# Up-projections of a hybrid decoder trunk as three fp32r products of rounded and low parts

## The chip, the cores and the metric

The kernel runs on one core of one Trainium2 chip. The metric is the device time of one launch in microseconds (us). PE is TensorE, PEld its weight loads, ACT is ScalarE, DVE is VectorE, POOL is GpSimd and SP is SyncE, which issues nearly all DMAs. A line such as L886 is a line of the kernel before.

## What is computed

A step of a two-layer recurrent decoder over 512 prompt tokens and 8 sample tokens (520 columns, held as two halves of 260). Each layer normalizes its input, projects it to four token mixers (A: RWKV-7, B: retention, C: RG-LRU, D: gated delta) and to 4 x 1024 merge-gate columns, runs the mixers, and merges them:

```python
h = rms_norm(x, lp['norm_g']) * (1.0 + scale[:, None]) + shift[:, None]
proj = jnp.einsum('btd,de->bte', h, lp['w_in'])
# oA, oB, oC, oD: mixer outputs, (tokens, 256) each, gated by silu of their own columns
branches = jnp.stack([oA, oB, oC, oD], axis=2)
up = jnp.einsum('btnw,nwd->btnd', branches, lp['w_up'])        # w_up: (4, 256, 1024)
gl = proj[..., OFF_G:].reshape(B, T, N_BRANCH, D_MODEL)
merged = jnp.sum(jax.nn.sigmoid(gl) * up, axis=2)
out = merged @ lp['w_out']
x_new = x + gate[:, None] * out
```

`up` is what the change touches. In each layer it is 4 branches x 8 column tiles = 32 tiles, each a 256-deep product for 128 output columns and 520 tokens.

## The kernel before

Everything lies channel-major: 128 channels on the partitions, 520 tokens along the free axis. Five engines run instruction lists written out by hand; one engine waits for another by a semaphore at a numbered step, and each engine works strictly in the order of its list. `L.tiles` gives the order of the weight tiles, and SP issues loads in the same order.

The large products (`proj` and `gate` tiles, the `out` tiles, and `ada`, the conditioning projection) are already computed from parts. `split` on ACT rounds a weight tile of 128x1024 to fp32r (L1436), POOL subtracts that from the tile in two halves of 128x512 (L708), and PE adds hi x hi, hi x lo and lo x hi (L836, L844) in 48 fp32r matmuls of 260 columns. The up tile idx (`up`, L877 to L888) is different: 4 matmuls in plain fp32 straight from the loaded weights `upw` (three buffers, `UP_RING`) and the mixer output in `RA`, `RB`, `RC` or `RD`. The trace shows two records for each such matmul, so 8 for an up tile. DVE then multiplies the result in PSUM by 1 + tanh of the gate and adds it to the merged sum (`merged`, L1888 to L1906: L1900 for idx below 8, else L1903 and L1904). Products on PSUM bank pairs alternate, so an up tile needs the pair that was used two tiles before. The tanh tiles of the gates are stashed in DRAM and brought back (`stash`, `bring_back`), again by SP.

The 32 up tiles of a layer are computed in three places. Tiles 0 to 7 (branch A) lie between gate tiles 8 to 15, while DVE and ACT prepare branch D: `first_out` and `gated(0)` finish branch A (L2063 to L2070, L1917 to L1921) in the middle of D's convolution (`conv`, L2079), after which come ACT's tanh (L1646), D's silu (L2097), a log series (`log1p`, L1825 to L1837) and a scan (L2108), for which PE waits at L1145. Tiles 8 to 17 (D and the first two of C) lie around the retention loop (`for c in range(NCB)`, L1326 to L1342 on PE), with two up tiles after each chunk and then the next gate tile. Tiles 18 to 31 (the rest of C, and B) are the tail of the layer: they alternate with `ada` tiles (14 of them in layer 0, 8 in layer 1), whose weights are 512 KB each; DVE merges, and for idx above 24 it also takes the low part of a merged tile (`m_lo`, L1886) after ACT has rounded it (`m_hi`, L1790). The `out` products follow. In the tail ACT's order is: for i in 0 to 13, `mod_rows(i)` (which splits the ada tile four ahead, once its load has landed) and from i = 7 on `m_hi(i - 7)`.

Of the kernel before, what the change touches and what calls it, by code (L numbers as in the profile page):

```python
# [18 lines left out]
P = 128  # L19
KT = D_MODEL // P  # L20
# [57 lines left out]
def build_program(nc, a, o, order):  # L78
# [8 lines left out]
    with ctx:  # L87
        def sb(name, shape, dt=F32):
            return ctx.enter_context(nc.sbuf_tensor(name, shape, dt))
# [22 lines left out]
        RC = sb("RC", [P, 4, TT])  # L112
# [4 lines left out]
        upw = sb("upw", [P, RING, 2, P])  # L117
# [8 lines left out]
        cT = sb("cT", [P, KT, 9])  # L126
# [15 lines left out]
        svA = sb("svA", [P, 6, NB, 2])  # L142
        svB = sb("svB", [P, 8, NB, 2])
        rowA = prow
        vecA = vecB = sb("vec", [P, 8, HD])
        vv = sb("vv", [P, 3, 16])
        so = sb("so", [P, 3, 16])
# [69 lines left out]
        class Layer:  # L217

            def __init__(self, n):
# [12 lines left out]
                    "pe_n", "act_n", "dve_n", "pe_m", "act_m", "dve_m")}  # L232
# [228 lines left out]
        for layer, L in enumerate(LAYERS):  # L461
# [354 lines left out]
            def _(pe):  # L816
# [50 lines left out]
                outs = (RA[:, 2:4, :], RB[:, 4:6, :], RC[:, 0:2, :], RD[:, 4:6, :])  # L867

# [68 lines left out]
                nc.tensor.transpose(psB[0:96, 0, 0:P], svA[:].rearrange("p n b i -> p (n b i)"), ident).then_inc(*ps_.step("rows"))  # L937
# [485 lines left out]
            def _(act):  # L1423
# [138 lines left out]
                def after_fill():  # L1562
                    evacs(fill_a.ends_in(next(slots)))
# [251 lines left out]
            def _(dve):  # L1815
# [247 lines left out]
                def first_out():  # L2063
# [6 lines left out]
                    gated(0, outs3[0], RA[:, 7:9, :])  # L2070

# [468 lines left out]
```

## Time and profile before

| | us |
|---|---|
| three runs | 1541.17, 1542.26, 1546.21 |
| median | 1542.26 |
| the profiled execution | 1549.12 |
| its span, first to last instruction | 1547.3 |

The profiled execution is 6.9 us over the median. PE is busy for 1429.0 us of the span (92%), DVE for 648.0, ACT for 519.4, POOL for 473.8; the granted clock of TensorE is 0.962 on average. An engine's busy share is a mean over the whole span. Whether a shorter product helps depends on who is awaited where it stands, so the time is read by the stretches of a layer. Layer 0's tiles 0 to 7 lie from 369 to 438 us, tiles 8 to 17 from 591 to 661 us and tiles 18 to 31 from 676 to 724 us; layer 1 repeats it some 750 us later.

### The profile page before, as it was taken

What the parts mean: (1) busy time and instruction counts of PE and PEld (TensorE: products, weight loads), DVE (VectorE), ACT (ScalarE), POOL (GpSimd) and SP (SyncE); (2) the same over time, 40 slices, a digit from 0 to 9 for tenths busy, and PEclk for the clock granted to TensorE, in tenths of its full rate; (3) what the DMA queues carried; (4) which work ended last, traced back from release to release, by engine and by line L of the source; (5) the groups of instructions that cost most, each with busy time, mean ns of one, the idle gap of its engine ahead of it and who ended that gap; (6) DMA issues with size and microseconds to landing.
All of it is one profiled execution on the core that took longest, in us unless ns stands there. A gap on an engine that the chain in (4) does not pass through costs nothing.

```text
span 1547.3 us, 33515 instructions
## 1 busy us (share of the span) xinstructions
PE 1429.0 (92%) x14880; PEld 1292.1 (84%) x14880; DVE 648.0 (42%) x1115; ACT 519.4 (34%) x780; POOL 473.8 (31%) x350
## 2 busy tenths in 40 slices
PE   6799999999899999897979999999999999989896
PEld 4699999888789888775879998998888988877695
DVE  5625313317732436545123541141494242563432
ACT  5524322234422234144333252221542123514322
POOL 0244322223221122157633442122422122212720
PEclk9899999999899999998999999999998999999998
DMA  9532321225231354477543323122352126246811
GB/s 319 192 92 67 83 64 49 57 56 120 74 95 41 66 112 122 94 244 230 162 127 95 82 68 83 43 56 56 83 126 82 43 57 118 75 117 169 274 43 55
DMA packets 275908, 162.18 MB, mean 105 GB/s; under 512 B 86102, under 2 KB 244922, under 8 KB 275252
## 3 DMA queue, kind: packets, MB, share of 16 engines
q1 hardware_dynamic: 274100, 159.06, 37.7%
q8 instruction: 117, 1.92, 0.5%
q10 hardware_dynamic: 1664, 0.98, 0.3%
q14 instruction: 27, 0.22, 0.0%
HBM read 135.25 MB, written 24.89 MB: 103 GB/s over the span
## 4 chain that ended last, share of the span: by engine, by line
PE 75%; DVE 14%; ACT 4%; issue 3%; DMA 2%; SPq 1%; POOL 0%; ACTq 0%; DVEq 0%
PE psA L836 31%; PE psA L844 15%; PE psA L886 5%; PE psB L772 3%; PE psB L781 3%; PE psB L782 2%; PE psB L717 1%; DVE RA L1930 1%; DVE ws L2079 1%; PE psB L959 1%; DMA RB<-in_ada_w 1%; PE psB L969 1%; DVE ws L1833 1%; PE psB L1145 1%; PE psB L1402 1%
## 5 line engine op out<-in xcount | busy, mean ns | idle before, releaser
L708 POOL TENSOR_TENSOR w_lo<-ring,w_hi 128x512 fp32r<-128x512 f32 (+1 forms) x274 | 382.2, 1417 | 956.8 <-ACT w_hi L1436 896.3
L836 PE MATMUL psA<-h_hi,w_hi 128*128 128x260 f32 x1984 | 430.9, 299 | 21.0 <-DVE h_lo L1848 12.8
L836 PE MATMUL psA<-h_lo,w_hi 128*128 128x260 f32 x1984 | 406.5, 287 | 0.0
L836 PEld LDWEIGHTS psA<-h_hi,w_hi 128*128 128x128 f32 x1984 | 312.6, 193 | 39.3 <-issue 19.8
L836 PEld LDWEIGHTS psA<-h_lo,w_hi 128*128 128x128 f32 x1984 | 312.9, 192 | 0.2
L844 PE MATMUL psA<-h_hi,w_lo 128*128 128x260 f32 x1984 | 275.2, 288 | 0.0
L844 PEld LDWEIGHTS psA<-h_hi,w_lo 128*128 128x128 f32 x1984 | 251.5, 189 | 4.6 <-issue 0.3
L1436 ACT CAST w_hi<-ring 128x1024 fp32r<-128x1024 f32 x133 | 137.2, 1033 | 33.3 <-PE psA L844 18.4
L787 ACT COPY ws<-psB 128x128 f32<-128x128 f32 x80 | 21.5, 268 | 246.5 <-PE psB L772 246.5
L795 DVE COPY_PREDICATED tg<-tmask,psB 128x128 f32<-128x128 uint8 x40 | 14.3, 356 | 137.5 <-PE psB L782 97.5
L1465 ACT ACTIVATE tg<-psA 128x520 f32<-128x520 f32 x48 | 28.9, 601 | 101.4 <-PE psA L844 101.2
L795 DVE COPY_PREDICATED ws<-tmask,psB 128x128 f32<-128x128 uint8 x40 | 14.3, 357 | 86.4 <-PE psB L782 51.2
L2323 DVE SCALAR_TENSOR_TENSOR xT<-psA,modT,xT 128x260 f32<-128x260 f32 x16 | 7.8, 489 | 97.2 <-PE psA L844 97.2
L708 POOL TENSOR_TENSOR w_lo<-ring,ra_lo 128x512 fp32r<-128x512 f32 x28 | 36.5, 1329 | 29.1 <-ACT ra_lo L1436 29.1
L886 PE MATMUL psA<-RB,upw 128*128 128x260 f32 x128 | 35.9, 434 | 8.4 <-DVE RA L1904 6.8
L886 PEld LDWEIGHTS psA<-RB,upw 128*128 128x128 f32 x128 | 27.1, 217 | 16.0 <-DVE RA L1904 7.3
L782 PE MATMUL psB<-tg,ws 64*64 64x32 f32 x640 | 38.0, 221 | 0.0
L782 PE MATMUL psB<-ws 64*64 64x32 f32 x640 | 37.4, 220 | 0.0
L886 PE MATMUL psA<-RA,upw 128*128 128x260 f32 x128 | 32.2, 399 | 4.4 <-DVE RA L1921 4.4
L708 POOL TENSOR_TENSOR rb_lo<-RB,ra_lo 128x512 fp32r<-128x512 f32 x20 | 25.5, 1303 | 31.9 <-ACT ra_lo L1436 31.9
L1762 ACT COPY RB<-psB 64x256 f32<-64x256 f32 x16 | 5.9, 367 | 85.3 <-PE psB L1342 85.2
L782 PEld LDWEIGHTS psB<-tg,ws 64*64 64x64 f32 x640 | 32.6, 137 | 1.1
(476 smaller groups left out, 2349.8 us busy)
## 6 DMA issues: line engine op xcount, KB each, us to landing
ring<-in_w_in SPq DMA_DIRECT2D x122, 512.0 KB, 4.1
scr_tanh<-tg SPq DMA_DIRECT2D x48, 260.0 KB, 4.5
ring<-in_ada_w SPq DMA_DIRECT2D x18, 512.0 KB, 4.3
upw<-in_w_up SPq DMA_DIRECT2D x64, 128.0 KB, 3.9
RA<-scr_tanh SPq DMA_DIRECT2D x30, 260.0 KB, 4.0
RB<-in_ada_w SPq DMA_DIRECT2D x14, 512.0 KB, 5.1
ws<-scr_tanh SPq DMA_DIRECT2D x24, 260.0 KB, 4.2
ring<-in_w_out SPq DMA_DIRECT2D x9, 512.0 KB, 4.6
```

Source lines behind the costliest of these rows:

```text
L708: nc.gpsimd.tensor_tensor(tile_part(RL[s][:, k], (kind, n)), tile_part(RS[s][:, k], (kind, n)), tile_part(HS[L.hslot[q]][:, k], (kind, n)) ...
L717: last = nc.tensor.matmul(psB[:, k, 0:HALF], bones, s4[:, k, :], start=True, stop=True)
L772: last = nc.tensor.matmul(meet(psB[sd(g), 2, q * CH:(q + 1) * CH], lv, 0), At[sd(g), q, :], meet(T4[sd(g), q, :], lv, 0), start=True, stop ...
L781: nc.tensor.matmul(meet(psB[sd(g), 2, q * CH:(q + 1) * CH], lv, 0), V4[sd(g), q, :], meet(Y4[sd(g), q, :], lv, 0), start=True, stop=True)
L782: last = nc.tensor.matmul(meet(psB[sd(g), 2, 256 + q * CH:256 + (q + 1) * CH], lv, 1), Y4[sd(g), q, :], meet(V4[sd(g), q, :], lv, 1), star ...
L787: nc.scalar.copy(meet(q64(Y), lv, 0), meet(q64(psB[:, 2, 0:256]), lv, 0)).then_inc(*ta.step("y"))
L795: nc.vector.copy_predicated(meet(q64(T), lv, 0), bc(meet(tmask[:, lv, :], lv, 0), 1, 4), meet(q64(psB[:, 2, 0:256]), lv, 0))
L836: nc.tensor.matmul(out(h), HS[L.hslot[q]][:, p, 0:m], cols(part(p), h), start=(p == 0 and part is hi), stop=False)
L844: last = nc.tensor.matmul(out(h), RL[s][:, k, 0:m], cols(hi(k), h), start=False, stop=(k == KT - 1))
L886: last = nc.tensor.matmul(out(hf), upw[:, idx % UP_RING, i, :], outs[MERGE[idx][0]][:, i, hf * HALF:(hf + 1) * HALF], start=(i == 0), stop ...
L1436: nc.scalar.copy(tile_part(HS[L.hslot[q]], SPLIT[q]), tile_part(RS[s], SPLIT[q])).then_inc(*aw.step("hi"))
L1465: A(half(th_tile(idx)), psA[:, b:b + 2, 0:HALF], ACT.Tanh, scale=0.5).then_inc(*am.step("th"))
```

## The change

`up` becomes three fp32r products, as the large tiles have them: 12 matmuls instead of 4. Their operands are new tiles: `up_hi` (weights rounded by ACT), `up_lo` (weights less `up_hi`, written over `upw`), and for each branch `out_hi` (ACT) and `out_lo`, each 128x1040, written behind the branch's gate.

- ACT rounds up weights 0 to 2 at the end of stage A (ahead of `mrow`), 3 to 20 behind the gate tiles of `ups_after`, and 21 to 31 in the tail, each behind `mod_rows(i)` and ahead of `m_hi`. From idx 3 on it waits for the load and for the up tile three before. It rounds the branch outputs behind gates 9, 23 and 28 and at i = 1 in the tail, ahead of the next `split`.
- POOL takes the low part of up weights 0 to 20 and of branch outputs 1 to 3, each ahead of one of its own gate or ada tiles. For branch 3 that is ada tile 5.
- DVE takes the low part of branch output 0, directly behind `gated(0)`, after waiting for ACT. In the tail it takes the low parts of up weights 21 to 31, each directly behind the merge three tiles before.
- To make room, some small tiles share memory: `svA` with `svB`, and `vv`, `so` and `cT` with each other.

```diff
-        upw = sb("upw", [P, RING, 2, P])
+        upw, uplo = sb_parts("upw", "up_lo", [P, RING, 2, P])
+        uphi = sb("up_hi", [P, RING, 2, P], F32R)
...
+            out_f = (RA[:, 2:4, :], RD[:, 4:6, :], RC[:, 0:2, :], RB[:, 4:6, :])
+            out_hi = (wsr[:, 8:10, :], mhi[:, 6:8, :], RClo[:, 2:4, :], RBr[:, 6:8, :])
+            out_lo = (RAlo[:, 2:4, :], mhi[:, 4:6, :], RClo[:, 0:2, :], RBr[:, 4:6, :])
+            ON_DVE = 21
...
+            ups_after = {10: (3,), 11: (4,), 12: (5,), 13: (6,), 14: (7,), 22: (8,), 23: (9,), 24: (10,), 25: (11,), 26: (12,),
+                         27: (13, 14), 28: (15, 16), 29: (17, 18), 30: (19, 20)}
+            outs_after = {9: (0,), 23: (1,), 28: (2,)}
+            two_on = lambda g: SPLIT[SPLACE["gate", g] + 2]
+            UPS_AT = {two_on(g): idxs for g, idxs in ups_after.items()}
+            UPS_AT[two_on(8)] = (0, 1, 2)
+            OUTS_AT = {two_on(g): bs for g, bs in outs_after.items() if g != 9}
+            OUTS_AT["ada", 5] = (3,)
...
             def _(pool):
                 for q, (kind, n) in enumerate(SPLIT):
                     s, _ = ring_slot(kind, n, L)
+                    for idx in UPS_AT.get((kind, n), ()):
+                        pool.wait_ge(*TR["act_u"].at("uhi", idx))
+                        nc.gpsimd.tensor_tensor(uplo[:, up_slot(idx)], upw[:, up_slot(idx)], uphi[:, up_slot(idx)], sub).then_inc(*pu.step("ulo"))
+                    for b in OUTS_AT.get((kind, n), ()):
+                        pool.wait_ge(*an.at("ohi", b))
+                        nc.gpsimd.tensor_tensor(out_lo[b], out_f[b], out_hi[b], sub).then_inc(*pu.step("olo"))
...
                 def up(idx):
-                    if idx in (0, 8, 16, 24):
-                        pe.wait_ge(*dn.at("gated", idx // 8))
+                    b, first = idx // 8, idx % 8 == 0
+                    if first:
+                        pe.wait_ge(*an.at("ohi", b))
                     psum_free("up", idx)
-                    pe.wait_ge(L.up[idx % UP_RING], 16 * (idx // UP_RING + 1))
-                    out = psum("up", idx)
+                    pe.wait_ge(*TR["act_u"].at("uhi", idx))
+                    out, s = psum("up", idx), up_slot(idx)
+                    for x in (out_hi[b], out_lo[b]):
+                        if x is out_lo[b] and first:
+                            pe.wait_ge(*(pu.at("olo", b - 1) if b else dn.at("olo")))
+                        for i in range(2):
+                            for hf in range(2):
+                                nc.tensor.matmul(out(hf), uphi[:, s, i, :], x[:, i, hf * HALF:(hf + 1) * HALF], start=(i == 0 and x is out_hi[b]), stop=False)
+                    pe.wait_ge(*low_at(idx))
                     for i in range(2):
                         for hf in range(2):
-                            last = nc.tensor.matmul(out(hf), upw[:, idx % UP_RING, i, :], outs[MERGE[idx][0]][:, i, hf * HALF:(hf + 1) * HALF],
-                                                    start=(i == 0), stop=(i == 1))
+                            last = nc.tensor.matmul(out(hf), uplo[:, s, i, :], out_hi[b][:, i, hf * HALF:(hf + 1) * HALF], start=False, stop=(i == 1))
                     last.then_inc(*pm.step("gate"))
...
+                def up_split(idx):
+                    act.wait_ge(L.up[up_slot(idx)], 16 * (idx // UP_RING + 1))
+                    if idx >= UP_RING:
+                        act.wait_ge(*pm.at("gate", idx - UP_RING))
+                    nc.scalar.copy(uphi[:, up_slot(idx)], upw[:, up_slot(idx)]).then_inc(*TR["act_u"].step("uhi"))
+                def out_split(b):
+                    act.wait_ge(*dn.at("gated", b))
+                    nc.scalar.copy(out_hi[b], out_f[b]).then_inc(*an.step("ohi"))
...
                         A(half(th_tile(idx)), psA[:, b:b + 2, 0:HALF], ACT.Tanh, scale=0.5).then_inc(*am.step("th"))
+                        for b in outs_after.get(idx, ()):
+                            out_split(b)
+                        for k in ups_after.get(idx, ()):
+                            up_split(k)
...
+                for idx in range(3):
+                    up_split(idx)
                 act.wait_ge(*pa.at("mt"))
...
                     if i < n_ada:
                         mod_rows(i)
+                    if i == 1:
+                        out_split(3)
+                    if 21 + i < 32:
+                        up_split(21 + i)
                     if i >= 7:
                         m_hi(i - 7)
...
                             T_(half(mg[j]), up, half(mg[j]), add).then_inc(*dm.step("mg"))
+                        if idx + 3 >= ON_DVE and idx + 3 < 32:
+                            s = up_slot(idx + 3)
+                            dve.wait_ge(*TR["act_u"].at("uhi", idx + 3))
+                            T_(uplo[:, s], upw[:, s], uphi[:, s], sub).then_inc(*du.step("ulo"))
...
                     gated(0, outs3[0], RA[:, 7:9, :])
+                    dve.wait_ge(*an.at("ohi", 0))
+                    T_(out_lo[0], out_f[0], out_hi[0], sub).then_inc(*dn.step("olo"))
```

## Rows read from the trace of the kernel before

**Rows 1.** The page: busy time of engines (part 1), chain of waits (part 4).

```profile
PE 1429.0 (92%) x14880; PEld 1292.1 (84%) x14880; DVE 648.0 (42%) x1115; ACT 519.4 (34%) x780; POOL 473.8 (31%) x350
PE 75%; DVE 14%; ACT 4%; issue 3%; DMA 2%; SPq 1%; POOL 0%; ACTq 0%; DVEq 0%
```

**Rows 2.** Windows: stretch, length, busy us, granted clock, DMA share, GB/s.

```profile
369.00:411.00 42.00, 36.11 (x248) 33.42 (x248) 38.67 (x48) 20.12 (x17) 13.55 (x9) 0.98 0.60 135
...
676.30:702.00 25.70, 23.31 (x106) 15.77 (x105) 11.04 (x16) 10.76 (x13) 22.35 (x18) 1.00 0.95 316
702.00:734.00 32.00, 22.04 (x88) 15.56 (x88) 20.26 (x23) 14.30 (x19) 25.52 (x18) 0.78 0.66 212
```

**Rows 3.** Timeline of PE, an up tile between gate tiles: start, us, idle before.

```profile
374.74 2.08 PE L844 MATMUL psA<-h_hi,w_lo 128*128 128x260 f32 x16
376.66 1.92 PE L886 MATMUL psA<-RA,upw 128*128 128x260 f32 x8
```

**Rows 4.** Timelines of ACT and PE, end of stage A.

```profile
343.63 1.04 ACT L1436 CAST w_hi<-ring 128x1024 fp32r<-128x1024 f32 x1
344.57 0.36 ACT L1629 COPY mrow<-psB 64x256 f32<-64x256 f32 x1
...
345.81 1.99 PE L717 MATMUL psB<-RA,cst 128*128 128x260 f32 x8 [1.62 <-ACT crow L1634]
```

**Rows 5.** Timelines of DVE and POOL around `gated(0)`.

```profile
358.98 1.24 DVE L2065 TENSOR_TENSOR RA<-RA,ws 128x1040 f32<-128x1040 f32 x1 [5.47 <-ACT ws L1488]
...
366.79 2.19 DVE L1921 SCALAR_TENSOR_TENSOR RA<-RA,ws 128x1040 f32<-128x1040 f32 x1
369.02 5.97 DVE L2079 SCALAR_TENSOR_TENSOR ws<-RD,parT,ws 128x510 f32<-128x510 f32 x6
...
360.39 7.49 POOL L708 TENSOR_TENSOR w_lo<-ring,w_hi 128x512 fp32r<-128x512 f32 x4 [13.14 <-ACT w_hi L1436]
```

**Rows 6.** Timelines of DVE, POOL and PE on to L1145.

```profile
397.18 0.69 DVE L1833 TENSOR_TENSOR ws<-ws 4x520 f32<-4x520 f32 x1
398.36 1.67 DVE L1833 TENSOR_TENSOR ws<-ws 4x520 f32<-4x520 f32 x1
...
398.16 3.02 POOL L708 TENSOR_TENSOR w_lo<-ring,w_hi 128x512 fp32r<-128x512 f32 x2 [6.37 <-ACT w_hi L1436]
...
411.23 3.75 PE L1145 MATMUL psB<-bg,cst 4*128 4x512 f32 x4 [4.49 <-DVE bg L2108]
```

**Rows 7.** Timelines of PE and ACT, second place and the gate before it.

```profile
573.16 0.60 PE L836 MATMUL psA<-h_hi,w_hi 128*128 128x260 f32 x2 [0.39 <-ACT ws L1732]
...
626.10 0.69 PE L1337 MATMUL psB<-ws,M 64*64 64x128 f32 x4 [4.11 <-DVE ws L2269]
...
644.76 3.67 PE L886 MATMUL psA<-RD,upw 128*128 128x260 f32 x16
...
645.73 0.60 ACT L1465 ACTIVATE tg<-psA 128x520 f32<-128x520 f32 x1
```

**Rows 8.** Up weight loads, issue to landing: up to 676 us, then 682 to 712.

```profile
DMA to landing us min/median/max: 2.2/3.3/5.0
...
DMA to landing us min/median/max: 3.8/6.4/7.7
```

**Rows 9.** Timelines of ACT, POOL, PE and DVE in the tails.

```profile
691.67 1.04 ACT L1436 CAST w_hi<-RB 128x1024 fp32r<-128x1024 f32 x1 [5.41 <-DMA RB<-in_ada_w]
...
690.19 2.53 POOL L708 TENSOR_TENSOR rb_lo<-RB,ra_lo 128x512 fp32r<-128x512 f32 x2
...
694.46 0.62 PE L1372 MATMUL psB<-rb_lo,c_parts 128*18 128x512 f32 x2
702.02 1.99 PE L886 MATMUL psA<-RB,upw 128*128 128x260 f32 x8 [0.39 <-DMA upw<-in_w_up]
...
711.74 1.34 DVE L1886 TENSOR_TENSOR ra_lo<-RA,merged_hi 128x520 fp32r<-128x520 f32 x1 [0.97 <-ACT merged_hi L1790]
1471.86 0.69 DVE L1886 TENSOR_TENSOR merged_lo<-mg,merged_hi 128x520 fp32r<-128x520 f32 x1
```

More of the change, by code:

```diff
@@ L111, in build_program @@
         RB, RBr = sb_parts("RB", "rb_lo", [P, 8, TT])
-        RC = sb("RC", [P, 4, TT])
+        RC, RClo = sb_parts("RC", "rc_lo", [P, 4, TT])
         RD, mhi = sb_parts("RD", "merged_hi", [P, 8, TT])
@@ L125, in build_program @@
         G = sb("G", [P, KT, 9])
-        cT = sb("cT", [P, KT, 9])
         chl = sb("c_parts", [P, KT, 18], F32R)
@@ L141, in build_program @@
         crowA = mg5[0:11, 2:4, :].rearrange("p a b -> p (a b)")[:, 0:7 * P]
-        svA = sb("svA", [P, 6, NB, 2])
         svB = sb("svB", [P, 8, NB, 2])
+        svA = svB[:, 0:6]
         rowA = prow
         vecA = vecB = sb("vec", [P, 8, HD])
-        vv = sb("vv", [P, 3, 16])
-        so = sb("so", [P, 3, 16])
+        decode_small = sb("decode_small", [P, 96])
+        vv, so = (decode_small[:, 48 * k:48 * k + 48].rearrange("p (n v) -> p n v", n=3) for k in range(2))
+        cT = decode_small[:, 0:72].rearrange("p (k s) -> p k s", k=KT)
         sa = sb("sa", [P, 2, 16])
@@ L231, in __init__ @@
                     "pe_c", "act_c", "dve_c", "pe_s", "act_s", "dve_s", "pe_p", "act_p", "act_w", "pool_w",
-                    "pe_n", "act_n", "dve_n", "pe_m", "act_m", "dve_m")}
+                    "act_u", "pool_u", "dve_u", "pe_n", "act_n", "dve_n", "pe_m", "act_m", "dve_m")}
                 self.n_ada = 24 if n == 0 else 8
@@ L476, in ada_bank, with low_at @@
                 return 2 if b in (1, 3) else 1
+            pu, du = TR["pool_u"], TR["dve_u"]
+            out_f = (RA[:, 2:4, :], RD[:, 4:6, :], RC[:, 0:2, :], RB[:, 4:6, :])
+            out_hi = (wsr[:, 8:10, :], mhi[:, 6:8, :], RClo[:, 2:4, :], RBr[:, 6:8, :])
+            out_lo = (RAlo[:, 2:4, :], mhi[:, 4:6, :], RClo[:, 0:2, :], RBr[:, 4:6, :])
+            up_slot = lambda idx: idx % UP_RING
+            ON_DVE = 21
+            def low_at(idx):
+                return pu.at("ulo", idx) if idx < ON_DVE else du.at("ulo", idx - ON_DVE)
             def merged_at(idx):
@@ L865, in proj @@
                         last.then_inc(*pp.step("proj"))
-                outs = (RA[:, 2:4, :], RB[:, 4:6, :], RC[:, 0:2, :], RD[:, 4:6, :])
                 def gate(idx, parts=range(PARTS)):
@@ L936, in _ @@
                 pe.wait_ge(*da.at("prep"))
-                nc.tensor.transpose(psB[0:96, 0, 0:P], svA[:].rearrange("p n b i -> p (n b i)"), ident).then_inc(*ps_.step("rows"))
+                nc.tensor.transpose(psB[0:96, 0, 0:P], svA.rearrange("p n b i -> p (n b i)"), ident).then_inc(*ps_.step("rows"))
                 pe.wait_ge(*as_.at("rows", 0))
@@ L2400 @@
     'pool_w0': 'lo lo lo lo lo lo lo lo lo lo lo lo lo lo lo lo lo lo lo lo lo lo lo lo lo lo lo lo lo lo lo lo lo lo lo lo lo lo lo lo lo lo lo lo lo lo lo lo lo lo lo lo lo lo lo lo lo lo lo lo lo lo lo lo lo lo lo lo lo lo lo lo lo lo lo lo lo lo lo lo lo lo lo lo lo lo lo lo lo lo lo lo lo lo lo lo lo lo lo lo lo lo lo lo lo lo lo lo lo lo lo lo lo lo lo lo lo lo lo lo lo lo lo lo lo lo lo lo lo lo lo lo lo lo lo lo lo lo lo lo lo lo lo lo lo lo lo lo lo lo lo lo lo lo lo lo lo lo lo lo lo lo lo lo lo lo lo lo lo lo lo lo lo lo lo lo lo lo lo lo lo lo lo lo lo lo lo lo'.split(),
+    'act_u0': 'uhi uhi uhi uhi uhi uhi uhi uhi uhi uhi uhi uhi uhi uhi uhi uhi uhi uhi uhi uhi uhi uhi uhi uhi uhi uhi uhi uhi uhi uhi uhi uhi'.split(),
+    'pool_u0': 'ulo ulo ulo ulo ulo ulo ulo ulo ulo ulo olo ulo ulo ulo ulo ulo ulo ulo olo ulo ulo ulo ulo olo'.split(),
+    'dve_u0': 'ulo ulo ulo ulo ulo ulo ulo ulo ulo ulo ulo'.split(),
     'pe_n0': 'mean var var var'.split(),
-    'act_n0': 'sq ln rn tz sq ln rn tz tz sq ln rn tz'.split(),
-    'dve_n0': 'cen normed gains bonus siluz gated normed siluz gated siluz gated normed siluz gated'.split(),
+    'act_n0': 'sq ln rn tz ohi sq ln rn tz ohi tz ohi sq ln rn tz ohi'.split(),
+    'dve_n0': 'cen normed gains bonus siluz gated olo normed siluz gated siluz gated normed siluz gated'.split(),
     'pe_m0': 'gl gl gl gl gl gl gl gl gl gl gate gl gate gl gate gl gate gl gate gl gate gl gate gate gl gl gl gl gl gl gl gl gl gate gl gate gl gate gate gl gate gate gl gate gate gl gate gate gl gl gate gate gate gate gate gate gate gate gate gate gate gate gate gate out out out out out out out out'.split(),
@@ L2428 @@
     'pool_w1': 'lo lo lo lo lo lo lo lo lo lo lo lo lo lo lo lo lo lo lo lo lo lo lo lo lo lo lo lo lo lo lo lo lo lo lo lo lo lo lo lo lo lo lo lo lo lo lo lo lo lo lo lo lo lo lo lo lo lo lo lo lo lo lo lo lo lo lo lo lo lo lo lo lo lo lo lo lo lo lo lo lo lo lo lo lo lo lo lo lo lo lo lo lo lo lo lo lo lo lo lo lo lo lo lo lo lo lo lo lo lo lo lo lo lo lo lo lo lo lo lo lo lo lo lo lo lo lo lo lo lo lo lo lo lo lo lo lo lo lo lo lo lo lo lo lo lo lo lo lo lo lo lo lo lo lo lo'.split(),
+    'act_u1': 'uhi uhi uhi uhi uhi uhi uhi uhi uhi uhi uhi uhi uhi uhi uhi uhi uhi uhi uhi uhi uhi uhi uhi uhi uhi uhi uhi uhi uhi uhi uhi uhi'.split(),
+    'pool_u1': 'ulo ulo ulo ulo ulo ulo ulo ulo ulo ulo olo ulo ulo ulo ulo ulo ulo ulo olo ulo ulo ulo ulo olo'.split(),
+    'dve_u1': 'ulo ulo ulo ulo ulo ulo ulo ulo ulo ulo ulo'.split(),
     'pe_n1': 'mean var var var'.split(),
-    'act_n1': 'sq ln rn tz sq ln rn tz tz sq ln rn tz'.split(),
-    'dve_n1': 'cen normed gains bonus siluz gated normed siluz gated siluz gated normed siluz gated'.split(),
+    'act_n1': 'sq ln rn tz ohi sq ln rn tz ohi tz ohi sq ln rn tz ohi'.split(),
+    'dve_n1': 'cen normed gains bonus siluz gated olo normed siluz gated siluz gated normed siluz gated'.split(),
     'pe_m1': 'gl gl gl gl gl gl gl gl gl gl gate gl gate gl gate gl gate gl gate gl gate gl gate gate gl gl gl gl gl gl gl gl gl gate gl gate gl gate gate gl gate gate gl gate gate gl gate gate gl gl gate gate gate gate gate gate gate gate gate gate gate gate gate gate out out out out out out out out'.split(),
```

## The prediction

> **What bounds the kernel now.** I read the page first: PE is busy 92% of the span and holds 75% of the chain of waits, DVE 14% [rows 1]. By that alone a shorter product on PE is time won. Then I asked, stretch by stretch, whom PE awaits where the up tiles stand, and that is another picture. In the first place (tiles 0 to 7) DVE is busy for 38.67 of 42 us [rows 2]: its list from `gated(0)` over the convolution, ACT's tanh and the log series to the scan is serial, and PE arrives early at its end and waits 4.49 us for the scan [rows 5, 6]. In the second place (8 to 17) PE waits 4.11 us for DVE's rows of the next chunk, the longest wait there [rows 7]; the rest is PE's own. In the third (18 to 31) the DMA engines are 95% busy at 316 GB/s over the first 25.7 us [rows 2], and an up weight lands 6.4 us after its issue where it took 3.3 before [rows 8]. So only a part of the up tiles stands where PE sets the end.
>
> **What PE itself gains.** A run of 16 fp32r matmuls starts at 374.74 and the next tile at 376.66: 1.92/16 = 0.120 us each. An up tile of plain matmuls has 8 records, listed as 1.92 us with the drain of the last; two in a row are listed as 3.67 us, so one more costs 3.67 - 1.92 = 1.75 us [rows 3, 7]. New: 12 x 0.120 = 1.44 us. That is 0.31 us per tile, 64 tiles, 19.8 us at most. By these rows a plain fp32 matmul costs 1.75/4/0.120 = 3.6 fp32r ones. (The Trainium skill, "FP8 and Floating Point Precision", TensorE Precision Notes, states four passes for true fp32; three products against four would be a quarter off each tile, 0.25 x 1.92 = 0.48 us and 31 us in all by that count, which the row does not bear out.)
>
> **End of stage A, tiles 0 to 2's weights.** ACT's list runs from a cast at 343.63 through `mrow` and two `crow` copies without a hole, and PE starts at 345.81 after waiting 1.62 us for the last of them [rows 4]. Three casts of 128x256 go ahead of `mrow`. The trace shows 1.04 us for 128x1024 and 0.36 for a copy of 256 columns [rows 4]; a quarter of the first, 0.26, and 0.5 bound one cast, and I take 0.33, near the 256-column row. Nothing covers them: PE's head sums, ACT's squares and `gated(0)` all come behind. **+1.0 us per layer** (0.8 to 1.5).
>
> **First place.** Before, PE starts up 0 right at the end of `gated(0)` (366.79 + 2.19) and DVE goes on with the convolution at 369.02 [rows 5]. Now DVE waits for ACT's cast of 128x1040 (1.04 for 1024 columns, with the hand-over 1.15) and then subtracts 1040 columns: 1.24 us alone, 2.19 beside POOL [rows 5]. POOL is busy there, and it has three more small subtractions ahead of a gate tile, so I take 2.0. Three further POOL subtractions (weights 3, 4, 5) fall ahead of its gate tiles while DVE is in the serial chain. A DVE instruction beside POOL grew from 0.69 to 1.67 us [rows 6]; so each costs DVE between 0 and 1.0, I take 0.4: +1.2. All of this goes through, for PE's wait of 4.49 us for the scan has no slack behind it on DVE: PE only waits longer, and its 5 shorter tiles before L1145 vanish in that wait. Tiles 5 to 7 lie behind it, where PE goes on without a wait: -0.94. Sum 1.15 + 2.0 + 1.2 - 0.94 = **+3.4 us per layer** (from 1.15 + 1.24 - 0.94 = 1.4 to 1.15 + 2.2 + 3.0 - 0.94 = 5.4).
>
> Beside it a rule of the Trainium skill ("SBUF — State Buffer", Who interferes with whom): a VectorE instruction with two inputs in SBUF contends with GpSimd's reads, and the loser of the shared port pair waits out the other's whole instruction. The trace agrees in that both stretch [rows 5, 6]; by a full wait each of the six small subtractions could cost DVE its own length, about 0.65 us, together 3.9.
>
> **Second place.** Ten tiles, 3.1 us on PE. Against it: weight 8's cast behind gate 22 stands ahead of the lru evacuation that PE already awaits for 0.39 us, +0.35 [rows 7]; branch output 1's cast and weight 9's stand ahead of the next lru evacuation, mostly in idle time of ACT, +0.2; POOL's longer turn stands beside DVE's rotary chain that frees up 9's banks, +0.4. Then branch output 2's cast and weight 15's stand behind the tanh of gate 28 at 645.73 + 0.60: weight 15 is ready near 647.7, but PE is through with the faster up 14 at 646.2 [rows 7]. A stall of 1.4 us where 0.1 was. Weight 17 behind gate 29 costs 0.4 in the same way. Where PE waits for DVE's rows [rows 7], the gain of the tiles before comes through only in so far as DVE's merges start sooner; I count 0.6 of the 3.1 as lost. 0.35 + 0.2 + 0.4 + 1.4 + 0.4 + 0.6 - 3.1 = 0.25, less the 0.1 that was there: **+0.2 us per layer** (-1.5 to +2).
>
> **Tail.** Three things. (1) POOL is busy 22.35 of 25.7 us [rows 2] with 2.5 us per ada tile; ada tile 5 was ready at 690.19 + 2.53 = 692.7 and PE asked for its low part at 694.46 [rows 9]. Branch output 3 (1040 columns, two halves' time, 2.5 us) goes ahead of it: 695.2, and up 24 stands behind. +0.8. (2) Three up weight buffers in a ring: up k has ended, its successor k + 3 is issued, lands 6.4 us later, and up k + 3 can run; PE already waited 0.39 us for one [rows 8, 9]. Now between landing and product stand ACT's cast (0.33, and up to 1.0 behind a weight split, which itself waits for a 512 KB load, as 5.41 us at 691.67 [rows 9]), DVE's subtraction, and one merge more, as DVE waits for the cast ahead of its next merge. Against it 0.31 of the shorter tile: between 0 and 1.1 us per three tiles, I take 0.4: 11 loads, some 3.7 rounds, +1.5. (3) For tiles 28 to 31 the low parts of weights stand in DVE's closing chain of merge and `m_lo` (0.69 alone, 1.34 beside POOL [rows 9]); 256 columns are half of that, 0.35 to 0.7 us, or more with a wait for ACT, four times: +1.5. Where PE ends sooner nothing comes of it, as its next product needs DVE's last low parts. (1) to (3) are 3.8; a slower pace lets the loads land sooner, which covers 0.8 of it in layer 0 and 0.3 in layer 1, where fewer loads are under way at the end: **+3.0 and +3.5** (bounds: -1 where the DMA engines alone set the pace and everything new hides under them, +8 each where all three add up).
>
> The shared small tiles bring no wait on this path; moved names alone cost nothing.
>
> **Sum.** 2 x 1.0 + 2 x 3.4 + 2 x 0.2 + 6.5 = 15.7 us. From the profiled execution, 1549.12 + 15.7 = 1564.8. That one lies 6.9 over the median of 1542.26, and the difference goes on the median: 1542.3 + 15.7 = **1558**. Uncosted: the granted clock was 0.78 from 702 to 734, where PE idles [rows 2]. Longer waits at up 0 and up 24 may bring more such stretches; at half clock 3 us of work cost 3 us more, and that sits in the upper range.
>
> **Rivals.**
> - *PE-bound after all.* The page's 92% speaks for it; the three places against it. If all DVE and ACT additions hid, the gain would be 19.8 us (1522). In a milder form stage A (+1.0) and the first place's lower bound (+1.4) are paid and the second place (-3.1) and the tail's 14 tiles (-4.3) won in full: 2 x -5.0 = -10.0, or 1532, which I give as its time. Chance 0.13.
> - *Even.* POOL's subtractions cost DVE nothing (first place +1.4), the tail hides in the DMA time (-1 each), the second place gives 1.5: 2 + 2.8 - 2 - 3 = -0.2, so 1542. Chance 0.13.
> - *The ring decides the tail.* Slower still: DVE waits for the cast of weight k + 3 before it merges tile k + 1, and up k + 3 needs the banks of tile k + 1. From landing to product that is 0.4 + 0.7 + 1.4 = 2.5 us where nothing stood, less 0.31, per three tiles. It decides from the point where landing (6.4 us) plus this exceeds the 8.3 us that three steps take when the ring is the limit (0.1 + 6.4 + 1.75). With 3.7 rounds it is 8 us per tail, 16 in all in place of 6.5: 1568. Against it: a slower pace empties the DMA queue, and 6.4 falls towards 3.3 [rows 8]. Chance 0.17.
> - *My forecast*, 1548 to 1566, chance 0.57.
> - *The change isn't what it says*: 12 matmuls per up tile and no plain fp32 pair must show; if not, no step above holds. No chance apart.
>
> **Numbers.** Slower by over 0.3% (over 1546.9): forecast and ring, 0.74. Within 0.3% (about what a measurement of this kernel can tell from no change): 0.13. Faster: 0.13. The range 1540 to 1572 leaves out most of the first rival below and some of the ring above; the forecast's own is 1548 to 1566.
>
> **What would show it.** 768 fp32r matmuls for up tiles at 0.120 us and none plain. The wait of L717's PE group for `crow` at 2.6 in place of 1.62. DVE idle some 1.1 us behind `gated(0)`, then a 1040-column subtraction of 1.2 to 2.2; PE's wait for the scan at 6 to 9 us in place of 4.49. A wait of 1.4 us on ACT at up 15. In the tail, DVE idle for ACT's casts between merges, and ada 5's low part later by 2.5. The forecast falls if DVE's stretch from `gated(0)` to the scan grows by under 2 us, if the tails (up 18 to the first `out` product) shrink, or if PE's waits in the second place stay as they are.

## The result, and the profile after

The changed kernel took 1568.63 us (median of 4 runs, 1566.68 to 1571.07), the kernel before 1544.24 beside it (4 runs): a ratio of 1.0157, 95% interval 1.0136 to 1.0178, 24.4 us slower. The forecast said slower, 1558 within 1540 to 1572; its sum was 15.7 us where 24.4 were paid. The time lies in that range, but above the 1548 to 1566 that the forecast gave as its own. The profiled execution of after took 1571.07 us (span 1569.3), 22 us more than that of before.

The page, busy time and chain, against [rows 1]: PE is busy 7 us less, DVE 38 more, POOL 63 more, and the chain moved from PE (75 to 71%) to DVE (14 to 16%).

```profile
PE 1422.1 (91%) x15136; PEld 1299.4 (83%) x15136; DVE 685.6 (44%) x1139; ACT 546.8 (35%) x852; POOL 536.4 (34%) x398
PE 71%; DVE 16%; ACT 5%; issue 4%; DMA 3%; POOL 1%; ACTq 1%; SPq 1%; DVEq 0%
```

I cut layer 0 at five instructions of PE that both kernels have: the transposes of the sample rows at the end of stage A, the first broadcast behind the scan, the transposes behind `prep`, the first ada product, and the modT product. Windows of before, then of after (us, busy PE, PEld, DVE, ACT, POOL, granted clock, DMA share, GB/s):

```profile
343.90:411.20 67.30, 57.41 (x411) 53.99 (x411) 54.17 (x63) 38.07 (x41) 24.25 (x15) 0.99 0.49 114
411.20:437.80 26.60, 26.57 (x168) 22.45 (x169) 13.94 (x25) 5.53 (x9) 7.32 (x6) 0.84 0.24 63
437.80:677.80 240.00, 227.27 (x2707) 204.43 (x2705) 101.03 (x186) 72.00 (x123) 48.95 (x37) 0.98 0.39 96
677.80:732.40 54.60, 42.25 (x179) 28.44 (x177) 31.24 (x38) 23.56 (x29) 47.87 (x36) 0.89 0.81 268
```

```profile
341.00:415.20 74.20, 57.90 (x432) 55.67 (x431) 59.02 (x64) 41.18 (x49) 34.69 (x23) 0.95 0.45 107
415.20:444.20 29.00, 29.00 (x181) 25.18 (x181) 12.90 (x25) 5.85 (x10) 5.19 (x5) 0.72 0.17 40
444.20:685.40 241.20, 225.73 (x2753) 205.40 (x2751) 105.61 (x187) 78.03 (x137) 67.45 (x54) 0.98 0.39 96
685.40:740.90 55.50, 39.30 (x229) 27.68 (x229) 43.07 (x49) 27.95 (x41) 51.34 (x37) 0.92 0.80 264
```

So +6.9, +2.4, +1.2 and +0.9; layer 1 has +6.7, +2.3, +0.7 and +1.4. Four fifths of it lie in the first two windows, which hold the end of stage A and the prediction's first place. The second window is the telling one: PE is busy throughout in both, has 0.93 us less to do, and takes 2.4 longer at a clock of 0.72 in place of 0.84.

Timelines of after around the first place (start, us, idle before and its releaser), against [rows 4 to 6]:

```profile
341.65 1.02 ACT L1491 CAST up_hi<-upw 128x256 fp32r<-128x256 f32 x3
343.82 1.99 PE L744 MATMUL psB<-RA,cst 128*128 128x260 f32 x8 [2.54 <-ACT crow L1684]
...
361.36 5.12 POOL L729 TENSOR_TENSOR up_lo<-upw,up_hi 128x256 fp32r<-128x256 f32 x3
364.24 1.66 DVE L1979 SCALAR_TENSOR_TENSOR RA<-RA,ws 128x1040 f32<-128x1040 f32 x1
367.10 1.73 DVE L2130 TENSOR_TENSOR ra_lo<-RA,ws_lo 128x1040 fp32r<-128x1040 f32 x1 [1.19 <-ACT ws_lo L1496]
398.98 0.91 POOL L729 TENSOR_TENSOR up_lo<-upw,up_hi 128x256 fp32r<-128x256 f32 x1 [5.06 <-ACT up_hi L1491]
399.32 1.12 DVE L1887 TENSOR_TENSOR ws<-ws 4x520 f32<-4x520 f32 x1
400.48 1.40 DVE L1888 TENSOR_SCALAR ws<-ws 4x520 f32<-4x520 f32 x1
401.91 1.67 DVE L1887 TENSOR_TENSOR ws<-ws 4x520 f32<-4x520 f32 x1
412.84 2.20 DVE L2168 TENSOR_TENSOR_SCAN bg<-cst,ws 4x520 f32<-4x520 f32 x1
415.19 3.75 PE L1177 MATMUL psB<-bg,cst 4*128 4x512 f32 x4 [7.30 <-DVE bg L2168]
```

The reader sees the casts ahead of `crow` (2.54 us for 1.62), DVE's wait of 1.19 and its subtraction of 1.73, three steps of the log series stretched while POOL works (0.69 and 0.42 alone; before has two such steps in a row, of which [rows 6] shows the first), and a scan of 2.20 us. The wait for the scan is 7.30 where it was 4.49.

An up tile is three groups of four, 1.44 us from one tile's start to the next:

```profile
441.31 0.64 PE L915 MATMUL psA<-ws_lo,up_hi 128*128 128x260 f32 x4
441.79 0.63 PE L915 MATMUL psA<-ra_lo,up_hi 128*128 128x260 f32 x4
442.26 0.64 PE L919 MATMUL psA<-ws_lo,up_lo 128*128 128x260 f32 x4
442.75 0.52 PE L915 MATMUL psA<-ws_lo,up_hi 128*128 128x260 f32 x3
```

Second place, the waits for DVE's rows and at up 15, against [rows 7]:

```profile
632.23 0.43 PE L1369 MATMUL psB<-ws,M 64*64 64x128 f32 x4 [4.83 <-DVE ws L2329]
654.01 1.20 PE L915 MATMUL psA<-merged_hi,up_hi 128*128 128x260 f32 x8 [0.47 <-ACT up_hi L1491]
```

Tail of layer 0, DVE's groups by shape (busy, mean ns, idle before), before and then after:

```profile
L1903 DVE SCALAR_TENSOR_TENSOR psA<-ws,psA 128x520 f32<-128x520 f32 x8 | 5.6, 697 | 8.6 <-PE psA L886 8.6
L1886 DVE TENSOR_TENSOR ra_lo<-RA,merged_hi 128x520 fp32r<-128x520 f32 x3 | 4.4, 1476 | 6.8 <-ACT merged_hi L1790 6.8
L1903 DVE SCALAR_TENSOR_TENSOR psA<-RA,psA 128x520 f32<-128x520 f32 x6 | 4.2, 700 | 6.1 <-PE psA L886 6.1
```

```profile
L1962 DVE TENSOR_TENSOR up_lo<-upw,up_hi 128x256 fp32r<-128x256 f32 x11 | 13.3, 1208 | 11.6 <-ACT up_hi L1491 11.6
L1957 DVE SCALAR_TENSOR_TENSOR psA<-ws,psA 128x520 f32<-128x520 f32 x8 | 5.5, 693 | 1.6 <-PE psA L919 1.6
```

### The profile page after: what moved, and what is told of

The parts are those of the page before. It is cut to its first block, busy times and chain, and to the rows that moved or that the text cites. A ratio compares the mean times of both kernels' runs of the same rounds, so it can differ in the third digit from the quotient of the medians.

```text
span 1569.3 us, 34231 instructions
## 1 busy us (share of the span) xinstructions
PE 1422.1 (91%) x15136; PEld 1299.4 (83%) x15136; DVE 685.6 (44%) x1139; ACT 546.8 (35%) x852; POOL 536.4 (34%) x398
## 4 chain that ended last, share of the span: by engine, by line
PE 71%; DVE 16%; ACT 5%; issue 4%; DMA 3%; POOL 1%; ACTq 1%; SPq 1%; DVEq 0%
PE psA L863 30%; PE psA L871 15%; PE psB L799 3%; PE psB L808 2%; PE psB L809 2%; PE psA L915 2%; DVE ws L2139 2%; PE psB L744 1%; DMA RB<-in_ada_w 1%; DVE RA L1988 1%; PE psB L991 1%; PE psA L919 1%; PE psB L1177 1%; DVE ws L1887 1%; PE psB L1001 1%
## 5 line engine op out<-in xcount | busy, mean ns | idle before, releaser
L863 PEld LDWEIGHTS psA<-h_lo,w_hi 128*128 128x128 f32 x1984 | 316.6, 195 | 0.2
L729 POOL TENSOR_TENSOR up_lo<-upw,up_hi 128x256 fp32r<-128x256 f32 x42 | 46.7, 1123 | 220.3 <-ACT up_hi L1491 220.3
L814 ACT COPY ws<-psB 128x128 f32<-128x128 f32 x80 | 21.5, 269 | 246.2 <-PE psB L799 246.1
L1509 ACT ACTIVATE tg<-psA 128x520 f32<-128x520 f32 x48 | 28.9, 602 | 106.7 <-PE psA L871 106.5
L2139 DVE SCALAR_TENSOR_TENSOR ws<-RD,parT,ws 128x511 f32<-128x511 f32 (+2 forms) x36 | 35.6, 1055 | 0.6 <-ACT ws L1686 0.6
L1482 ACT COPY RA<-psA 128x520 f32<-128x520 f32 x18 | 10.7, 594 | 67.6 <-PE psA L871 62.4
L1962 DVE TENSOR_TENSOR up_lo<-upw,up_hi 128x256 fp32r<-128x256 f32 x22 | 22.7, 1034 | 25.4 <-ACT up_hi L1491 25.4
```

Source lines behind the costliest of these rows:

```text
L729: nc.gpsimd.tensor_tensor(uplo[:, up_slot(idx)], upw[:, up_slot(idx)], uphi[:, up_slot(idx)], sub).then_inc(*pu.step("ulo"))
L863: nc.tensor.matmul(out(h), HS[L.hslot[q]][:, p, 0:m], cols(part(p), h), start=(p == 0 and part is hi), stop=False)
L2139: last = STT(out[:, t, sh:SEQ], raw[:, t, 0:SEQ - sh], par(wname, tap * n + t), out[:, t, sh:SEQ], mult, add)
```

## The experiments

Each time below is set against the kernel before, run on the same chip between them; by that measure after is +24.4 us.

**Which branches pay.** The edit, with the plain product and wait of before for a branch in `PLAIN`, and its casts and subtractions left out:

```
+ PLAIN = (0,)     # (1, 2, 3), (0, 1) and (0, 1, 2, 3) in the other three
  def up(idx):
+     if b in PLAIN:
+         ...fp32: upw x out_f, 4 matmuls
+         return
```

> The changed kernel with branch 0 (tiles 0 to 7 of both layers) back in plain fp32; branches 1 to 3 stay three products. Theory A (the cost sits in the first place, in VectorE's chain to the scan and in the lower granted clock behind the longer wait for it, with 0.9 us at the end of stage A): the two traces stand 0.9 + 5.9 + 2.3 us apart per layer there, so this kernel comes back by about 18 us, to 1550. Theory B (the ring of split weights and GpSimd's small subtractions in the tail are the cost): little comes back, about 1565. Theory C (the cost is spread over all tiles, as by a lower clock or by the number of instructions): a quarter of 24 us comes back, 1562.

Measured: 1555.47, +11.7 (1.0077, 1.0056 to 1.0097).

> Only branch 0 as three products; tiles 8 to 31 in plain fp32. Theory A: nearly the whole cost is here, 1544 + 18 = 1562. Theory B: 1547 or less. Theory C: 1544 + 6 = 1550. If first place and the rest add up, this kernel and the one with branch 0 plain stand as far above the kernel before, together, as the changed kernel does (24 us).

Measured: 1560.81, +17.0 (1.0108, 1.0083 to 1.0132). Its first two windows last as long as in after, 74.2 and 28.9 us; with branch 0 plain they are those of before, 67.4 and 26.9.

> Branches 0 and 1 (tiles 0 to 15) in plain fp32, branches 2 and 3 (tiles 16 to 31: the end of the second place and the whole tail) as three products. The traces show 1.2 and 1.35 us per layer in the tail. Theory A: 1544 + 3 = 1547. Theory B: 1544 + 15 or more, 1560. Theory C: half of 24 us, 1556. What lies between this kernel and the one with branch 0 alone plain is branch 1: 0.8 us per layer by the traces.

Measured: 1551.28, +7.5 (1.0056, 1.0035 to 1.0076): between theory A and theory C. Its tails last 57.7 and 48.6 us where before has 54.6 and 43.5.

> The changed kernel with all four branches in plain fp32: what is left of the change is the places in memory (shared small tensors, the low parts' regions) and no added instruction. All theories: same as before, 1544 within 0.2%. If it is slower by several us, a wait from the shared small tensors is part of the cost, which no theory has.

Measured: 1544.04, +0.2 (1.0000, 0.9986 to 1.0015).

The layout is free. Branch 0 costs 13 (after less its plain version) to 17 us, and 17.0 + 11.7 overshoots 24.4 by 4.3, about what the intervals allow. Theory A has the larger part, but the rest costs 7 to 12 us (after less branch 0 alone, or branch 0 plain) where it said 6; theory B is out for branch 0, theory C fits neither end. Branches 2 and 3 alone cost 7.5 where theory A had 3: the tail is not free, though the pair of traces above shows little there.

**What lengthens DVE's chain.** Branch 0's low part moved to GpSimd:

```
- dve.wait_ge(*an.at("ohi", 0))
- T_(out_lo[0], out_f[0], out_hi[0], sub).then_inc(*dn.step("olo"))
+ OUTS_AT: b = 0 on POOL, ahead of gate 10's low parts
```

> The changed kernel with the low part of branch 0's output on GpSimd, ahead of gate 10's low parts, and nothing of it on VectorE: VectorE neither waits for the rounded part (1.2 us) nor subtracts (1.7 us), TensorE gets the low part some 1.5 us later. Theory A: the chain to the scan is 2.9 us shorter per layer and the clock loses less, 6 to 9 us off, 1560 to 1563. Rival (VectorE's chain grew by contention, not by these two): 1567 to 1570.

Measured: 1565.67, +21.9 (1.0138, 1.0120 to 1.0156), between theory and rival; the interval overlaps that of after, so the windows have to carry the reading. The first window fell from 74.2 to 70.0 us (69.5 in layer 1), the wait for the scan to 2.67 (2.00). The second stayed at 29.1, at clock 0.72:

```profile
409.88 1.23 DVE L2166 TENSOR_TENSOR_SCAN bg<-cst,ws 4x520 f32<-4x520 f32 x1
411.26 3.75 PE L1177 MATMUL psB<-bg,cst 4*128 4x512 f32 x4 [2.67 <-DVE bg L2166]
```

GpSimd's small subtractions taken away (`if idx < KT`: no subtraction, the third product reads `uphi`):

> The changed kernel without the low parts of the weights of tiles 0 to 7; their third product reads the rounded weights instead, so TensorE does as many matmuls as before (the outputs lack these terms). GpSimd has eight small subtractions fewer per layer, beside VectorE's chain to the scan. The prediction priced their contention with VectorE at 1.2 us per layer: 2 to 3 us off, 1566. If contention is the main cost of the first place: VectorE's chain is 3 us shorter or more per layer, 1560 or less. If they touch nothing: 1568.6.

Measured: 1562.1, +18.3 (1.0127, 1.0105 to 1.0148). The first window is 70.5 us (71.0 in layer 1), the scan 1.23, DVE's 1040-column subtraction 1.24. The time lies between the two that the expectation set apart:

```profile
365.92 1.24 DVE L2133 TENSOR_TENSOR ra_lo<-RA,ws_lo 128x1040 fp32r<-128x1040 f32 x1 [1.19 <-ACT ws_lo L1499]
...
407.78 1.23 DVE L2171 TENSOR_TENSOR_SCAN bg<-cst,ws 4x520 f32<-4x520 f32 x1
409.16 3.75 PE L1180 MATMUL psB<-bg,cst 4*128 4x512 f32 x4 [4.81 <-DVE bg L2171]
```

GpSimd's small subtractions cost DVE's chain 3.7 us in layer 0 and 3.2 in layer 1. The forecast had 2.0 for them: 1.2 for weights 3 to 5, and 0.8 in the subtraction of 1040 columns, taken as 2.0 where it is 1.24 alone. Moving the low part of branch 0 off DVE gave 4.2 and 4.7. The two overlap (7.9 together in layer 0, where the window less stage A grew by 6.0). The rule that I set beside the sum (the Trainium skill, "SBUF — State Buffer", Who interferes with whom: the loser of the shared port pair waits out the other's instruction) gave 3.9 for six of them; these runs agree with it more than with my 2.0.

**The clock.** 44 matmuls in PE's wait for the scan, nothing moved:

```
+ pe.wait_ge(*aw.at("hi", SPLACE["gate", 14]))
+ for k in range(44):
+     nc.tensor.matmul(psB[:, 3, 0:HALF], HS[...][:, k % KT, :], hhi[:, k % KT, 0:HALF], start=True, stop=True)
  pe.wait_ge(*dd.at("gc"))
```

> The changed kernel with 44 matmuls of 128 x 260 (single pass, 0.12 us each, 5.3 us in all) into an unused PSUM bank inside TensorE's 7.3 us wait for the scan; no work is moved and nothing waits for them longer than today. If the idle wait is what the lower granted clock follows (20.5 us at half clock there in each layer, 10.2 before): half of 7 to 10 us per layer, 7 to 10 us off in all, 1559 to 1562. If the clock falls whatever the engine does in the wait: 1568 to 1570.

Measured: 1562.4, +16.5 (1.0118, 1.0093 to 1.0142), 7.9 us off after by the medians; the two intervals overlap at their ends, so here too the windows carry the reading. Second window of both layers (the wait for the scan is 1.96 us, the broadcast behind it 1.98 in place of 3.75):

```profile
413.60:436.80 23.20, 23.15 (x180) 21.00 (x181) 12.94 (x25) 5.85 (x10) 5.29 (x5) 0.93 0.20 50
1171.10:1197.40 26.30, 26.29 (x181) 23.58 (x181) 12.93 (x25) 5.84 (x10) 5.28 (x5) 0.81 0.18 45
```

The chain to the scan is as long as in after (74.1 us); work of no use in the wait gave 5.8 and 2.7 us back behind it. The granted clock splits this. It has two levels here, full and half (2.4 and 1.2 GHz). In after it is half until 9.2 us behind the start of the first broadcast, and again from 16.0 to 22.9 us. Here the first stretch is 3.4 us in both layers; the second is gone in layer 0 and stays, 6.8 us, in layer 1. In before the first stretch lasts until 8.6 us (9.0 in layer 1), as in after, and there is no second. So what after has over before is the second stretch: 6.9 us at half clock, 3.4 us of work. It does not follow the length of the wait. After's two stretches, then layer 1's second window with branch 0's low part on GpSimd, and without the small subtractions:

```profile
415.20:424.40 9.20, 9.20 (x30) 7.08 (x31) 6.13 (x11) 0.00 (x0) 0.91 (x1) 0.50 0.00 0
431.20:438.10 6.90, 6.90 (x29) 5.86 (x28) 4.54 (x11) 2.28 (x4) 0.95 (x1) 0.51 0.23 75
1171.80:1201.20 29.40, 29.38 (x180) 26.06 (x181) 13.56 (x25) 8.58 (x14) 8.77 (x7) 0.71 0.21 52
1171.00:1196.60 25.60, 25.60 (x181) 22.31 (x181) 13.87 (x25) 5.85 (x10) 6.68 (x5) 0.83 0.21 50
```

With the low part on GpSimd the waits for the scan were 2.67 and 2.00 us, shorter than the 4.49 and 3.52 of before, and the clock was 0.72 and 0.71. Without the small subtractions they were 4.81 and 5.36, and the clock 0.72 and 0.83: after the longest wait of these four the second stretch is missing, and the window is 1.2 us shorter than that of before (26.8), about what the three shorter tiles were to give (0.94). Shown, then, is that work in the wait shortens the first stretch of half clock behind the broadcast, by 5.8 us in each layer, some 2.9 us of time. What brings the second is not shown. It stood in all six layers with three products and an unedited first place (after, branch 0 alone, and the next kernel), and in two of eight with plain tiles there, 3.4 us long; whether the products themselves bring it is a rival that no run separates.

**The tail.** DVE's low parts of weights 21 to 31 taken away in the same manner:

> The changed kernel without the low parts of the weights of tiles 21 to 31, which VectorE makes between its merges; their third product reads the rounded weights (the outputs lack these terms), so TensorE does as many matmuls. In the tail TensorE waits 16.0 and 12.9 us for VectorE's merges and more (12.4 and 7.6 before). If VectorE's extra 0.7 us per tile is what holds the tail: 11 x 0.7 = 7 us per layer are at stake, of which some 3 to 5 come back: 1558 to 1563. If TensorE there waits for the ring or for ScalarE's casts: 1567 to 1569.

Measured: 1568.57, +22.7 (1.0145, 1.0124 to 1.0166): nothing to tell from after. DVE is busy 32.3 us in place of 43.1, and the windows are no shorter (layer 1's is 1.3 us longer), at a lower clock:

```profile
685.80:741.20 55.40, 39.92 (x229) 29.40 (x229) 32.30 (x38) 28.05 (x41) 49.98 (x37) 0.86 0.79 264
1446.70:1492.90 46.20, 35.00 (x198) 27.94 (x197) 23.90 (x32) 20.88 (x33) 32.22 (x25) 0.86 0.79 248
```

PE's waits for merges fell from 8.1 to 3.5 us (11.0 to 7.6 in layer 1). In layer 0 its waits for POOL's low parts grew from 1.7 to 3.1, that for `modT` from 6.5 to 8.6, and half clock lasted 15.9 us where after has 9.3. So taking these 13 us of DVE work away brought no time; that they cost nothing at an equal clock is not shown, and why the clock is lower (0.86 for 0.92 and 0.96) stays open.

**Filling the wait with real work.** First seven of gate 14's parts (five in the kernel before):

```
+ gate(14, range(7))
  pe.wait_ge(*dd.at("gc"))
```

> The changed kernel with seven of gate 14's twelve parts ahead of TensorE's wait for the scan, and gate 13's tanh on ScalarE ahead of its wait for the sums of k, so that gate 14's PSUM is free by then. VectorE waits 7.3 us and more behind the first broadcast today, so a broadcast that comes no later than the scan costs nothing. Theory A (the wait for the scan and the lower clock behind it are most of the first place): the 7.3 us wait per layer is filled and the clock falls less behind it, 2 x (7 + 2 to 4) = 18 to 22 us off, 1547 to 1551. Rival (VectorE's chain after the scan, not TensorE's idle time, sets the end of this stretch): the wait comes back at the second broadcast or at the transposes behind prep, 1564 to 1569. Rival on the clock (it falls by itself, whatever the waits): 14 us off, 1554.

Measured: 1563.71, +19.9 (1.0133, 1.0114 to 1.0152).

> The kernel before with the same edit, five parts of gate 14 ahead of the wait for the scan, which is 4.5 us there (3.5 in layer 1). Theory A: 2 x (4 + 1 to 3), 10 to 14 us off, 1530 to 1534. Rival (VectorE's chain after the scan sets the end): 1542 to 1544. Rival on the clock: 8 off, 1536.

Measured: 1543.42, -0.4 (0.9997, 0.9983 to 1.0010). Both are at their rivals' times. I had taken a part for 0.96 us; it is 0.48, so PE's waits there (two in each kernel) only fell to 4.48 and 2.53 us together, and the second window kept a clock of 0.72 and 0.79.

Then all of it, with half of gate 15 between the broadcasts:

```
+ gate(14)
  pe.wait_ge(*ad.at("lnk")); pe.wait_ge(*dd.at("gc"))
  ...
- gate(14)
  up(5)
+ gate(15, range(6))
  pe.wait_ge(*dd.at("ar"))
  ...
- gate(15)
+ gate(15, range(6, PARTS))
- ACT: gates(12) ... wait ks ... gates(13, 14)
+ ACT: gates(12, 13) ... wait ks ... gates(14)
```

> The changed kernel with the whole of gate 14 ahead of the wait for the scan (gate 13's tanh ahead of ScalarE's wait for the sums of k), and half of gate 15 between the two broadcasts, so that no wait of TensorE is left from tile 4 to the transposes behind prep. All of gate 14 is 5.8 us; with seven parts (3.4 us) ahead the kernel came down by 4.9 us. Theory A: 2 x (5.8 + 1 to 3 of clock), 1550 to 1555. Rival (VectorE's chain from the scan to prep, 24 us, sets the end of the stretch): 1563, as with seven parts.

Measured: 1562.02, +16.2 (1.0109, 1.0090 to 1.0129). This is the rival's time. The first two windows:

```profile
338.60:414.20 75.60, 62.39 (x479) 59.97 (x479) 60.41 (x64) 43.16 (x52) 37.16 (x25) 1.00 0.47 109
414.20:435.80 21.60, 19.73 (x133) 17.15 (x133) 13.89 (x25) 4.01 (x7) 4.23 (x3) 0.76 0.16 41
1096.80:1172.40 75.60, 63.62 (x480) 61.42 (x479) 60.44 (x64) 43.14 (x52) 36.74 (x25) 0.98 0.47 109
1172.40:1196.90 24.50, 23.03 (x133) 19.73 (x133) 13.86 (x25) 4.01 (x7) 4.19 (x3) 0.65 0.13 35
```

Layer 0 gained 6.0 us over after's 103.2, layer 1 3.1: DVE's chain is too long for gate 14 to cover (PE still waits 2.98 us for the scan), and behind it the clock is 0.76 and 0.65.

> The kernel before with the same edit. Five parts ahead gave nothing (1543.4): the idle time fell by 2 us and half of the stretch's clock was lost elsewhere. Theory A: the whole 4.5 us wait is gone and the later stretch is denser, 1533 to 1538. Rival (VectorE's chain or the clock takes it back again): 1542 to 1544.

Measured: 1535.33, -10.5 (0.9933, 0.9913 to 0.9953), faster than both kernels. First two windows of both layers:

```profile
343.80:413.00 69.20, 63.11 (x459) 59.84 (x459) 56.11 (x63) 38.67 (x43) 27.21 (x16) 1.00 0.48 115
413.00:434.60 21.60, 19.73 (x120) 16.10 (x121) 13.04 (x25) 4.81 (x8) 4.36 (x3) 0.84 0.27 73
1090.70:1160.50 69.80, 64.59 (x460) 61.16 (x459) 56.63 (x63) 38.25 (x41) 24.27 (x16) 0.98 0.47 114
1160.50:1181.30 20.80, 20.03 (x120) 16.51 (x121) 12.88 (x25) 5.54 (x9) 4.61 (x4) 0.84 0.27 65
```

Together 90.8 and 90.6 us where before had 93.9 and 94.3: two thirds of the gain. The rest lies outside these windows, in part in a second place of 237.3 us in layer 1; I did not separate it.

## Why the prediction was right in sign and short in size

- **PE's own price** was exact: 1.44 us per tile. It says nothing of the time, as forecast.
- **End of stage A**: +1.0 forecast, the wait for `crow` grew by 0.92. Right.
- **First place**: +3.4 forecast, 8.4 paid in layer 0 (6.9 + 2.4 - 0.9 of stage A), 8.1 in layer 1. This is the step that was short, in two terms. (1) The stretch up to the scan was 4.35 (1.15 + 2.0 + 1.2) and came to 6.0. The wait for the cast (1.19) and the subtraction by itself (1.24) were well sized; POOL's contention was not. Its small subtractions were 2.0 (0.8 + 1.2) and cost 3.7 and 3.2. I counted three of them in DVE's chain behind the 1040-column subtraction; that of weight 6 came too, right ahead of the scan. Behind that subtraction the chain grew by 4.2 us: 1.7 in the convolution, 1.1 in the log series, 0.4 ahead of the scan and 1.0 on it; against it two instructions ahead of the wait became 1.1 us shorter (2.22 and 2.19 to 1.67 and 1.66), which no term had (4.2 - 1.1, with 0.5 on the subtraction itself, is 3.6, close to the 3.7 that taking the small ones away gave). (2) The lower clock was left at zero and named as uncosted. The clock of the second window fell from 0.84 to 0.72, and the -0.94 of the three tiles turned into +2.4: 3.3 us per layer, the second stretch of half clock. The forecast had a row with clock 0.78 beside PE's idle time [rows 2] and tied the risk to longer waits. The wait did grow, from 4.49 to 7.30, but the same clock stood behind waits of 2.67 and 2.00: by the length of the wait it could not have been priced.
- **Second place**: +0.2 forecast, +1.2 and +0.7 in this pair of traces. Over all eight traces with three products there against five with plain ones it is 241.2 for 239.05 in layer 0 and 240.7 for 238.7 in layer 1: +2.0. The stall at up 15 is 0.47 in place of 1.4; the waits for DVE's rows grew, 4.11 to 4.83.
- **Tail**: +3.0 and +3.5 forecast, +0.9 and +1.4 in the pair; but over eight traces with three products there (all but the one without low parts) against the five with plain ones it is 56.4 for 53.9 in layer 0 and 45.1 for 43.5 in layer 1, +2.5 and +1.7, and branches 2 and 3 alone cost 7.5. So it was somewhat over-priced in layer 1, and the direction was right. PE's waits for DVE's merges, before and after in layer 0:

```profile
PE psA L886 <- DVE RA L1904: 2.2, 1, 2.2
PE psA L886 <- DVE mg L1904: 0.6, 1, 0.6
PE psA L915 <- DVE mg L1958: 5.3, 4, 2.4
PE psA L915 <- DVE RA L1958: 2.8, 3, 1.3
```

  They grew from 2.8 to 8.1 us, and from 4.6 to 11.0 in layer 1, against the 4.3 us that 14 shorter tiles save. What may have softened it, argued and not tried by itself, is a row that I had not asked for: DVE stood idle there for 21.5 us in waits of the three groups shown, and the low parts, at 1.2 us each twice what I gave them, and DVE's 11.6 us of waits for ACT's casts can go into that. Term (1) did not come: PE waited 1.7 us in all for POOL's low parts, 1.4 before.
- **The rivals**: "the ring decides the tail" has the measured time, 1568, and the wrong place; in layer 0 no cast of the tail's up weights waited for a load, in layer 1 two did, 6.4 us together, and the tail cost less than the 8 us that this rival gives it. That its time is the measured one is luck. "PE-bound" and "even" are out.
- The sign "the forecast falls if the tails shrink" did not come; "the wait for the scan at 6 to 9 us" did, 7.30 and 7.32; the wait of 1.4 us at up 15 was 0.47.

Over all traces, then, the first place was short by 9.7 us in two layers and the second place by 3.6, and the tail was 2.3 over; that the time lay within 1540 to 1572 owes something to the tail's excess.

Open: windows add up to 22 of 24.4 us, and single executions of one kernel differ by 5 us either way with their mean granted clock (19 runs of before: 1538.7 to 1548.5). The mean clock was 0.967 over these and 0.959 over after's 4. How much of branches 1 to 3's 7 to 12 us is clock and how much waits is not settled within 2 us per layer.

## What to carry to other kernels

An engine with 92% busy time still has stretches in which it arrives early; a change that takes work from it and puts work on the engine it waits for lengthens that wait. Look at the granted clock behind it too: here it cost another 3.3 us per layer, by a cause that is only in part known. Price the contention of a second engine on the whole serial chain, instruction by instruction, not only on the ones newly added. Before adding work to the engine awaited, look whether independent work of the waiting engine can stand in the wait: here that edit alone, without the change, gave 10.5 us. Read a stage from several traces: one pair showed a tail of +0.9 where eight against five showed +2.5.

## What the runs showed of the hardware

- A GpSimd subtraction of 128 x 256 is 0.73 to 0.91 us where VectorE is light and 1.7 to 3.2 beside its long two-input instructions: 1.12 us on the mean of 42. The same on VectorE beside GpSimd: 1.2 us on the mean of 11, 0.58 to 2.15.
- A VectorE instruction of 4 partitions is stretched as much as one of 128: the scan of 4 x 520 is 1.23 us alone and 2.20 beside GpSimd.
- TensorE's clock fell to half behind the first broadcast in every kernel, while the engine worked. In the changed kernel it fell again 1.1 us into the second broadcast, with PE busy since the first (0.50 over 9.2 us, 1.00 over 6.8, 0.51 over 6.9).
- In the last two kernels PE was busy but for short waits, and the window behind the scan, with broadcasts that use 4 of the 128 rows, still had a clock of 0.65 to 0.84. What of it these broadcasts do was not tried by itself.
